# Startup of a two-block transformer kernel on Trainium2: 32 matmuls of zeros, constants loaded behind slot 2, and GpSimd's squares of x and the mem load placed behind the low parts of x

## What is computed

```python
for i in range(DEPTH):
    x = x + 0.5 * swiglu(rmsnorm(x, ffn1_norm[i]), ffn1_w_gate[i], ffn1_w_up[i], ffn1_w_down[i])
    h = rmsnorm(x, mix_norm[i])
    ...
    o_mem = memory_cross_attention(q_mem, rmsnorm(mem, mem_norm[i]), mem_w_kv[i], memq_norm[i], memk_norm[i])
    x = x + jnp.concatenate([o, o_mem], axis=-1) @ w_out[i]
    x = x + 0.5 * swiglu(rmsnorm(x, ffn2_norm[i]), ffn2_w_gate[i], ffn2_w_up[i], ffn2_w_down[i])
```

## Time and profile before

| | us |
|---|---|
| median of 3 runs (2139.41 to 2140.47) | 2140.39 |
| the profiled execution's own time | 2141.11 |
| its span, first to last instruction | 2139.3 |
| TensorE matmuls busy | 2072.3 (97%) |
| VectorE busy | 1277.7 (60%) |
| ScalarE busy | 1030.1 (48%) |
| GpSimd busy | 120.3 (6%) |
| mean granted TensorE clock | 0.990 of full |

### The profile page before, as it was taken

How to read it: one execution, slowest core, us unless ns; L and a number is a source line. 1 busy time by engine, 2 the same in 40 slices (tenths; PEclk the granted TensorE clock), 3 DMA queues, 4 the chain that set the end, 5 groups by cost and what they waited for, 6 DMA issues and landing times.

```text
span 2139.3 us, 39735 instructions
## 1 busy us (share of the span) xinstructions
PE 2072.3 (97%) x16726; PEld 2017.7 (94%) x16748; DVE 1277.7 (60%) x1144; ACT 1030.1 (48%) x975; POOL 120.3 (6%) x83
## 2 busy tenths in 40 slices
PE   7999999999999998899999999999998999999997
PEld 6999998999999997699999999999998999999996
DVE  6556655655665667456557556755445666665445
ACT  5445645534443366344436454544345563545343
POOL 4000000100100002020000001010001000001001
PEclk9999999999999999899999999999999999999999
DMA  6555443455465544035545344435553443554452
GB/s 252 198 192 177 166 170 118 162 193 190 163 217 182 191 163 155 37 139 206 195 176 197 138 158 158 178 123 212 180 192 120 159 162 136 187 186 158 177 194 80
DMA packets 51562, 360.32 MB, mean 168 GB/s; under 512 B 5632, under 2 KB 7808, under 8 KB 8320
## 3 DMA queue, kind: packets, MB, share of 16 engines
q1 hardware_dynamic: 50768, 355.18, 45.8%
q0 software_dynamic: 688, 3.60, 0.5%
HBM read 357.71 MB, written 1.05 MB: 168 GB/s over the span
## 4 chain that ended last, share of the span: by engine, by line
PE 92%; DVE 4%; ACT 2%; issue 1%; POOL 0%; DMA 0%; ACTq 0%; SPq 0%; DVEq 0%; POOLq 0%
PE ps L236 25%; PE ps L237 25%; PE ps L238 25%; PE ps L283 2%; PE ps L285 2%; PE ps L284 2%; PE ps L272 1%; DVE wlo L232 1%; PE ps L267 1%; PE ps L268 1%; PE ps L585 1%; ACT whi L227 1%; PE ps L1486 1%; PE ps L1478 1%; DVE in_lo L440 1%
## 5 line engine op out<-in xcount | busy, mean ns | idle before, releaser
L232 DVE TENSOR_TENSOR wlo<-raw,whi 128x2048 fp32r<-128x2048 f32 x335 | 783.0, 2339 | 520.0 <-ACT whi L227 519.0
L236 PE MATMUL ps<-in_hi,whi 128*128 128x256 f32 x3708 | 1050.5, 283 | 10.8 <-DVE wlo L232 4.9
L237 PE MATMUL ps<-in_lo,whi 128*128 128x256 f32 x3708 | 1039.2, 280 | 0.0
L238 PE MATMUL ps<-in_hi,wlo 128*128 128x256 f32 x3708 | 1038.5, 280 | 0.0
L227 ACT ACTIVATE whi<-raw 128x2048 fp32r<-128x2048 f32 x335 | 638.4, 1908 | 238.3 <-PE ps L238 214.0
L236 PEld LDWEIGHTS ps<-in_hi,whi 128*128 128x128 f32 x3708 | 701.9, 189 | 18.6 <-issue 5.3
L237 PEld LDWEIGHTS ps<-in_lo,whi 128*128 128x128 f32 x3708 | 702.3, 189 | 2.1 <-issue 1.4
L238 PEld LDWEIGHTS ps<-in_hi,wlo 128*128 128x128 f32 x3708 | 701.9, 189 | 0.0
L236 PE MATMUL ps<-h_hi,whi 128*128 128x256 f32 x960 | 270.9, 282 | 0.0
L237 PE MATMUL ps<-h_lo,whi 128*128 128x256 f32 x960 | 269.8, 281 | 0.0
L238 PE MATMUL ps<-h_hi,wlo 128*128 128x256 f32 x960 | 269.4, 281 | 0.0
(11 more groups left out here) (251 smaller groups left out, 1728.9 us busy)
## 6 DMA issues: line engine op xcount, KB each, us to landing
raw<-in_slots SPq DMA_DIRECT2D x335, 1024.0 KB, 4.8
ws<-in_mem_t POOLq DMA_DIRECT2D x2, 1024.0 KB, 8.5
consts<-in_consts SPq DMA_DIRECT2D x1, 1600.0 KB, 13.2
consts<-in_consts POOLq DMA_DIRECT2D x1, 1472.0 KB, 6.7
x<-in_x_t SPq DMA_DIRECT2D x1, 1024.0 KB, 7.6
y_t<-x SPq DMA_DIRECT2D x1, 640.0 KB, 3.4
y_t<-x SPq DMA_DIRECT2D x1, 384.0 KB, 3.7
params<-in_params SPq DMA_DIRECT2D x1, 105.0 KB, 14.5
```

Of the source, the lines that this page charges most:

```text
L232: dve.tensor_tensor(wlo[:, j], raw[:, j], whi[:, j].bitcast(F32), ALU.subtract).then_inc(lo_ready, 1)
L236: pe.matmul(out, whi[:, j, o:o + n], hi, start=start, stop=False, skip_group_check=True)
L237: pe.matmul(out, whi[:, j, o:o + n], lo, start=False, stop=False, skip_group_check=True)
L238: return pe.matmul(out, wlo[:, j, o:o + n], hi, start=False, stop=stop, skip_group_check=True)
```

## The change

It adds 32 matmuls of zeros to TensorE's program in front of the first block, into the bank `gate_ps` that the gate block on slot 2 later starts anew. It moves the loads of the constants and of `params2` on SP's queue from behind slot 1 to behind slot 2. And on GpSimd it replaces the wait for `params` and x by a wait for all eight low parts of x (`fin_lo`), and puts the load of mem behind the squares of x.

```diff
+WARM = 32
...
                 sp.dma_start(raw[:, j], d_slots[j]).then_inc(raw_full[j], 16)
                 if j == 0:
                     sp.dma_start(x[:, :, :], d_x.rearrange("(k p) t -> p k t", p=P)).then_inc(loaded, 16)
-                if j == 1:
-                    sp.dma_start(consts[:, :], d_consts[0]).then_inc(consts_loaded, 16)
-                    sp.dma_start(params2[:, :], d_params2).then_inc(consts_loaded, 16)
+            sp.dma_start(consts[:, :], d_consts[0]).then_inc(consts_loaded, 16)
+            sp.dma_start(params2[:, :], d_params2).then_inc(consts_loaded, 16)
             with sp.Fori(1, SLOTS // RING) as i:
...
         @block.gpsimd
         def _(pool):
-            pool.wait_ge(loaded, 32)
+            pool.wait_ge(fin_lo, DT)
+            pool_ffn_in(pool, 0, x_tile(0))
             pool.dma_start(mem, d_mem.rearrange("(k p) t -> p k t", p=P)).then_inc(mem_loaded, 16)
-            pool_ffn_in(pool, 0, x_tile(0))
             pool_mem_squares(pool)
             pool_mix_squares(pool, 0)
...
         @block.tensor
         def _(pe):
             pe.wait_ge(consts_set, 2)
+            for _ in range(WARM):
+                pe.matmul(gate_ps, zeros[:, 0:P], zeros[:, :], start=True, stop=True, skip_group_check=True)
             for n, (f1, m, f2, out) in enumerate(STAGES):
```

## The result

The changed kernel takes 2144.04 us (median of 22 runs, 2142.02 to 2148.37) against 2140.44 us (22 runs, 2137.29 to 2143.10): **ratio 1.0017, 95% interval 1.0011 to 1.0024, so 3.6 us slower** (2.4 to 5.1). The forecast was 5.2 us slower, in a range of 2142.0 to 2147.8. The profiled execution took 2144.94 us by itself, with a span of 2143.1.

What follows compares the result with a forecast made beforehand. TensorE, 92% of the chain, was taken as the bound, so only its standstills count. x's sum -0.2 (absorbed), mem's sum +4.8 and clock +0.4 gave +5.2 on 2140.4: 2145.6 us, range 2142.0 to 2147.8.

Steps and rivals of the forecast that it cites:

- the likeliest case: Waits before x's and mem's sums on TensorE make the kernel 4.4 to 6.3 us slower, 2144.8 to 2146.7; chance 0.48.
- the second case: At the start, mem lands in 4.8 us or a late slot 3 means fewer turns: 2142.9 to 2144.6; chance 0.33.
- Low parts of x, warm-up, constants: Start: low parts done at 13.6, warm-up at 11, slots 1 to 3 split before 26; TensorE 5.9 us earlier.
- GpSimd's squares of x: Begun at 13.7, 8.2 us undisturbed, stretched by three slot splits to 28.3; TensorE, ready at 22.6, stands 5.7 us.
- The turn-by-turn model: GpSimd tensor operations and VectorE ones with two SBUF inputs alternate by whole instructions; a slot split costs 2.29 us.
- The mem load: On GpSimd's queue, issued at 28.25 instead of 9.56, 6.1 us from issue to landing, landed at 34.4.
- Squares of mem: On GpSimd from 34.4, 8.2 us plus 3.0 of turns, less 0.2: done 45.4 against 40.60 wanted, shift +4.8 us.
- The clock: TensorE at half speed after the new gaps delays the chain from mem's sum: bounds 0 and 0.9 us, 0.4 added.
- From the start to the whole time: TensorE is nearly continuous after 48.80, so what is won or lost by then arrives at the end.
- faster: Splits don't stop GpSimd's squares, x's done at 21.8, mem's at 36.2: shift -4.4, 2136.0; chance 0.05.
- slow load: Mem's load takes 10.9 us as first use of GpSimd's queue: shift 6.8 to 7.7, 2147.2 to 2148.1; chance 0.14.
- no change that can be told: Quicker mem load or fewer turns on GpSimd leave the time within 0.2%, 2142.9 to 2144.6; chance 0.33.

Runs made afterwards that it cites:

- the two last versions: Changed kernel with x's and mem's sums moved behind gate blocks: 2136.85 us; the same plus 14 matmuls of zeros before down block 0: 2136.36 us.
- the two in which ScalarE was stuck: Changed kernel with mem's sum moved behind down block 1: 2150.11 us; the same with x's sum also behind the gate block on slot 2: 2145.75 us.

## Why the prediction was right, step by step

The direction was right, 3.6 us lies in the range, and the two waits came where they were forecast. The size was less good. 2144.04 lies under the likeliest case's own range (2144.8 to 2146.7) and inside that of the second case (2142.9 to 2144.6), although what the second case stands for, a load of 4.8 us or fewer turns, did not happen. The time alone would have pointed to the wrong case; the rows tell them apart.

**Low parts of x, warm-up, constants.** As said: eight low parts in 3.25 us, the warm-up over at 10.1 (11 forecast), slot 3's high half begun at 20.77 (21.4 forecast). The gain that these would have given, 5.9 us, was there on TensorE (the second block ended near 22.7, the forecast said 22.6), and it was given back at x's sum, as forecast.

**GpSimd's squares of x.** Forecast 28.3, measured 27.88. The turn-by-turn model held to half a microsecond, whichever order the first two products took: in one execution they ran 13.61 to 17.7 with a split between, in others (the run without warm-up) both before it, and the last sum ended between 27.7 and 28.0 in each. Of the 0.4 us, 0.1 is the earlier start of the series; the rest is taken to be small overlaps at the turns. The Trainium skill's SBUF — State Buffer, section Who interferes with whom, says that a VectorE operation with two SBUF inputs contends with a GpSimd one that reads SBUF, and that the port they share is an exclusive lock. The trace agrees: the product issued at 23.30, behind the split of slot 3, took 3.09 us, and one without a split beside it 1.03.

**The mem load.** Forecast 6.1 us from issue to landing, measured 6.35 (27.67 to 34.02). The slow first load was traffic, not first use: the same load took 8.4 us in the run with GpSimd's edit alone and 9.7 us in that with half the squares, issued at 20.97 into slot loads. The 4.4 us of the second case, an estimate by the fit in the Trainium skill's DMA: Bandwidth & Descriptors, section Anatomy of one DMA, was seen in no run; the shortest here is 6.1.

**Squares of mem.** Forecast 8.2 us and 3.0 us of turns from the landing, 11.0 in the net; measured 44.6 - 34.1 = 10.5. With the two terms before it that puts mem's sum at 44.64 against 45.4: +4.0 where the forecast said +4.8. The shift of mem's sum was oversized by 0.8 us, some 0.4 of it in this term and the rest because mem had landed 0.3 us before the forecast's 34.35.

**The clock.** Both gaps went with half clock. I had added 0.4 us for slower matmuls in mem's sum; the row shows 0.1 (1.13 against 1.02). Instead the half clock fell on down block 0, which I had taken as hidden behind ScalarE's and VectorE's chain: it ended at 53.7, the split of slot 5 at 52.8. It had less room than I gave it. I set 5.5 us against 7.2 and left out the matmuls of zeros ahead of it (0.8 us in the kernel before, 1.5 in the changed one); in the kernel before TensorE stood only 0.64 us before slot 5:

```profile
48.80 0.38 PE L236 MATMUL ps<-in_hi,whi 128*128 128x256 f32 x1 [0.64 <-DVE wlo L232]
```

So a term of 0.9 us came in where I had none, and slot 5 is at +4.9, where my sum had +5.2. That these are so close is partly luck: 0.8 us too much in the wait and 0.3 in mem's sum stand against 0.9 too little in the down block.

**From the start to the whole time.** My assumption was that a shift at 48.80 arrives unchanged at the end. In the profiled executions +4.9 became +3.8, in the medians +3.6. Adding up the stretches at half clock between 60 and 2120 us gives 34.1 us in the kernel before and 30.7 in the changed one, which is worth up to 1.7 us at half rate; the same stretches (27.3 and 37.5 us) go with the odd order of the two last versions' own times, 2136.44 for the one with slot 5 at 45.74 and 2140.07 for the one with 44.60. Over eleven of the profiled executions (all but the two in which ScalarE was stuck) the time from slot 5 to the end goes with these stretches, from 2086.1 us with 23.9 us of them to 2093.7 with 37.5, some 0.4 us for each us. It is not the whole: two executions with the same 37.5 us took 2091.1 and 2093.7. That the stretches are the cause of the 1.1 us is argued and was not tested. The forecast had named time gone after 60 us as a sign of being wrong, and about 1 us did go there: the assumption that a shift at 48.80 arrives unchanged is the step that held worst.

The rivals: "faster" fell with GpSimd's rows, its squares of x ending at 27.7 and not before 24; "slow load" fell with 6.35 us; "no change that can be told" has the measured time in its range, but the change can be told. My bound of 4.3 us was too wide: the interval of 22 runs reaches only some 1.4 us to each side and excludes no change.

## What to carry to other kernels

Before an operation is moved behind another on a side engine, follow its result to the engine that bounds, and its place in that engine's program: GpSimd's 8 us of squares of x were free as long as they ran before TensorE wanted them, and became the critical path when they were moved by 3 us and their port had other users. If an early start gains nothing, move the consumer too, and put it behind the block whose end the next step of the third engine waits for anyway: that turned +3.6 us into -3.0. Count a moved DMA by what it is moved past, here 18 us, and not by its own length.

## What the runs showed of the hardware that was not expected

TensorE's clock fell to half behind short gaps. In the run with the mem load first 2.08 us without work before x's sum were enough (half clock from 26.4 to 29.8), in the changed kernel 2.46 us before mem's sum (from 45.8 to 49.2). The length of a gap alone does not decide it: in the run with GpSimd's edit alone, 3.03 us before x's sum were followed by full clock until 43.9. And in the changed kernel's first gap (5.16 us) and the 3.41 us of the version with both sums behind gate blocks, the stretch at half clock began inside the gap.

The same 1 MB load from GpSimd's queue took between 6.1 and 13.5 us: 6.2 to 6.8 in the seven executions that issued it near 28 us with slot 2 ahead of the constants, 8.4 near 28 us with the constants in their old place, 9.7 at 20.97, and 10.9 to 13.5 in the four that issued it before 10 us, while the first slots and the constants were loading.

And of GpSimd's first two products one split of VectorE came between them in some executions and behind them in others, with no effect on when the series ended.
